# Deferring the norm's factor: branch projections of the raw x, scaled on VectorE afterwards

## The chip, the cores and the metric

The kernel runs as one program on one core of a Trainium2 chip. The metric is the device time of one execution in microseconds (us). Three runs of the kernel before gave 3948.61, 3948.72 and 3963.4 us, median 3948.72 us. One further execution was recorded by the profiler.

## The reference, cut to what matters

Two blocks run after each other on x (1024 tokens, width 1024). The change lies where the first hands x to the second.

```python
x = x + gate[:, None] * y                    # end of the first block, y = (...) @ w_out[1]

def rmsnorm(x, g):
    return x * lax.rsqrt(jnp.mean(x * x, axis=-1, keepdims=True) + RMS_EPS) * g

h = rmsnorm(x, g_mix)                        # start of the second block
z = h @ w_in                                 # the branch projections
q, k, v, f = split(z[..., :FOX_COLS])        # q, k: rmsnorm per head of 64; f: 8 logits
zr = z[..., FOX_COLS:FOX_COLS + RWKV_COLS]
zr = zr + mu_shift * (token_shift(zr) - zr)  # needs the token before
r, kr, vr, dw, da, dg = split(zr)
decay = exp(-exp(-softplus(-(w0 + tanh(dw) @ w_decay_up)) - 0.5))
a = sigmoid(a0 + da @ w_aaa_up)
kk = kr * k_k / max(sqrt(sum(kr * k_k squared)), 1e-12)     # per head
kr = kr * (1 + (a - 1) * k_a)
bonus = sum(r * kr * r_k) * vr
gates = sigmoid(z[..., FOX_COLS + RWKV_COLS:])              # 2048 columns
```

The norm's factor is one number per token, so it can be applied to x ahead of the product or to the product's output.

## The kernel before

All arrays lie feature-major: 128 features on the partitions, tokens along the free axis. Every float32 operand of a large product is parted into a rounded high part and a low rest, and a product is three matmuls: high by high, high weights by low x, low weights by high x. A tile of 128 output features takes 8 parts of x (k), two halves of 512 tokens (c) and three matmuls, 48 in all.

**End of the first block.** `gemm_residual` multiplies eight tiles of `w_out`. Per tile VectorE adds the result to x (L502), ScalarE stores x (L529) and squares it (L533), and VectorE adds the squares up (L494). After the last tile TensorE takes the mean of the squares per token (L471), ScalarE the root (L538), VectorE the reciprocal (L516). `end_section` (L159) then holds all engines together.

**Start of the second block.** `branches` begins in `norm`. TensorE spreads the factor over the partitions (L2588), ScalarE copies it to SBUF (L2680), VectorE makes u = x * gain * factor (L2785), ScalarE rounds u (L2683), VectorE (L2788) and GpSimd (L2568) subtract for the low part. SyncE loads the first weight tiles (L2521), then some twenty small operands (L2526), for which VectorE waits. GpSimd parts the weight tiles (L2562, L2564). TensorE fills its wait with `keep_busy` matmuls (L166).

**The 84 chunks.** 42 tiles (4 value, 4 query, 4 key, 14 "shifted" for the rwkv branch, 16 gates) make 84 chunks of 512 tokens, numbered s = 0 to 83, with 24 matmuls each. A list written out by hand, `order`, gives every engine the same sequence: `gemm` s, what is set "after" it, `keep` s, what is set "late" after it. A chunk's four psum regions are reused every fourth chunk, so `gemm` s waits for `keep` s-4. GpSimd parts tile j+2 after both chunks of tile j are multiplied.

In `keep` ScalarE empties the psum: for value, query and key by one copy; for a shifted chunk by a copy to `raw` (L2701) and a scaled copy (L2702), after which VectorE adds the shifted part (`shift`, L2816); for a gate by a sigmoid (L2708), which SyncE stores.

Eight **preparations** i = 0 to 7 of the rwkv operands begin at chunk s = 34 + 3i. TensorE: `low` after chunk s (L2642), `ksum` after s+1 (L2650), `rksum` after s+4 (L2655). ScalarE: in `rates`, late in s, a square and two sigmoids (L2740 to L2743); in `decay`, late in s+1, a root (L2746) and three exponentials (L2751 to L2753). VectorE: in `rates` a running sum and a subtraction (L2822, L2824); in `decay` a maximum, a reciprocal (L2831), kk (L2833) and four more (L2836 to L2841); in `products`, late in s+2, one product (L2847); in `bonus`, late in s+4, one product (L2851). GpSimd: in `products` four products (L2574 to L2580), the first of which waits for kk.

Of the kernel before, what the change touches and what calls it, by code (L numbers as in the profile page):

```python
# [21 lines left out]
P = 128  # L22
# [187 lines left out]
class Ahead:  # L210


    def __init__(self, pg, st, nk, tiles):
        self.pg, self.tiles = pg, tiles
        self.raw = pg.sbuf(st, "weights", [P, 2, nk, P])
        self.hi, self.lo = pg.pair(st, "weights", [P, 2, nk, P])

    def begin(self):

        self.loaded = [self.pg.sem("ahead_loaded") for _ in range(2)]  # L220
        self.rounded, self.parted = self.pg.sem("ahead_rounded"), self.pg.sem("ahead_parted")

    def fetch(self, queue):
        for b in range(2):
            queue.dma_start(self.raw[:, b], self.tiles(b)).then_inc(self.loaded[b], 16)

# [195 lines left out]
def gemm_residual(pg, cn, w_of, n, rhs, x, parts, nk, store=None, squares=None, maker_in=None, beside_in=None, x_source=None, ahead=None):  # L422
# [7 lines left out]
    with ExitStack() as st:  # L430
        w = Weights(pg, st, nk, ahead)
        maker = maker_in(st) if maker_in else None
        beside = beside_in(st) if beside_in else None
        acc_ready, acc_free, stored = pg.sem("acc_ready"), pg.sem("acc_free"), pg.sem("stored")
# [5 lines left out]
        with nc.Block() as block:  # L440
            @block.sync
            def _(sp):
# [12 lines left out]
                elif maker:  # L455
                    with sp.Fori(1, n // 2) as i:
                        for b in range(2):
                            sp.wait_ge(w.parted, 2 * i + b + 1)
                            sp.dma_start(w.raw[:, b], in_turn(w_of)(i, b)).then_inc(w.loaded[b], 16)

            @block.tensor
            def _(pe):
                multiply(pg, pe, w, rhs, pg.acc, chunks, nk, acc_ready, acc_free, n, maker=maker, beside=beside)
                if squares:
# [10 lines left out]
            def _(pool):  # L475
# [3 lines left out]
                part_weights(nc, pool, w, acc_ready, n)  # L479

            @block.vector
            def _(dve):
# [13 lines left out]
                for t in range(n):  # L496
                    dve.wait_ge(acc_ready, t + 3)
# [7 lines left out]
                    if squares and t >= 2:  # L505
# [5 lines left out]
                if squares:  # L511
# [8 lines left out]
            def _(act):  # L520
# [5 lines left out]
                for t in range(n if store is not None or squares else 0):  # L526
# [9 lines left out]
                if squares:  # L536
                    act.wait_ge(mean_ready, 1)
                    nc.scalar.activation(pg.rstd[:, 0:width // P], pg.aux[:, 0, 0:width // P], ACT.Sqrt, bias=cn["eps"][:]).then_inc(rms_ready, 1)  # L538
                if store is not None:
                    act.wait_ge(stored, 16 * n)  # L540
# [1527 lines left out]
def first_block(pg, cn, x_dram, arena):  # L2068
# [3 lines left out]
    with ExitStack() as both:  # L2072
# [23 lines left out]
        for l in range(DEPTH):  # L2096
# [10 lines left out]
            with early, ExitStack() as feats:  # L2107
                h = pg.pair(feats, "h", [P, KD, TOK])
# [3 lines left out]
                if not last:  # L2112
# [4 lines left out]
                              beside_in=None if last else next_in, ahead=ahead)  # L2117
            pg.end_section()

# [263 lines left out]
def branches(pg, cn, x, names, cols, conv, ops, tail, end_decay, minus_c, drams):  # L2383
# [63 lines left out]
    for s in range(n_first, 2 * n):  # L2447
        j, c = divmod(s, 2)
        order.append(("gemm", s))
        order += at_slot.get((s, "after"), [])  # L2450
        order.append(("keep", s))
        if kinds[j][0] == "shifted":
            order.append(("shift", s))
            if j < first_shifted + 2:
                order.append(("squash", s))
# [10 lines left out]
    with ExitStack() as st:  # L2466
        hi, lo = pg.pair(st, "h", [P, KD, SEQ])
        raw_w = pg.sbuf(st, "weights", [P, 2, KD, P])
        w_hi, w_lo = pg.pair(st, "weights", [P, 2, KD, P])
# [3 lines left out]
        sig, rate, total, cur, inv, prev, sq = (temps[:, i] for i in range(7))  # L2473
        bonus = tail[:, 0:2 * BANK].rearrange("p (r n) -> p r n", n=BANK)
# [8 lines left out]
        u, rstd_all = ops[:, 1:3], tile(3)  # L2483
# [6 lines left out]
        x_scaled, x_rounded, even_parted, odd_parted = pg.sem("x_scaled"), pg.sem("x_rounded"), pg.sem("even_parted"), pg.sem("odd_parted")  # L2490
# [3 lines left out]
        raw_ready, shifted, squashed = pg.sem("raw_ready"), pg.sem("shifted"), pg.sem("squashed")  # L2494
# [4 lines left out]
        bonus_stored = [pg.sem("bonus_stored") for _ in range(2)]  # L2499
# [1547 lines left out]
```

## Time and profile before

| | us |
|---|---|
| median of three runs | 3948.72 |
| profiled execution, its own time | 3957.22 |
| span of its trace | 3955.3 |
| TensorE busy | 3662.7 (93%) |
| VectorE busy | 2009.4 (51%) |
| GpSimd busy | 1862.1 (47%) |
| ScalarE busy | 1210.5 (31%) |

Read the busy shares as averages over stages with different limits. The stage that the change touches runs from about 1769 us (last section of the first block) to about 2382 us (end of `branches`). A row of a timeline is: start, duration, engine, line, operation, output<-inputs, count, and in brackets the idle time ahead of it with what ended it. Float32 matmuls on unparted operands appear as two records each.

### The profile page before, as it was taken

The page shows a single profiled execution, that of the slowest core. Times are in us where ns is not written, and L with a number is a line of the kernel's source. Part 1 is how long each engine was busy: PE and PEld are TensorE (multiplying, and loading weights), DVE is VectorE, ACT ScalarE, POOL GpSimd, SP SyncE. Part 2 cuts the span into 40 slices and gives each one's busy share as a digit, 9 for nine tenths or more (in the row PEclk, how much of TensorE's full clock was granted, in tenths as well). Part 3 has the DMA queues.
Part 4 walks back from the last instruction along what each step waited for, and adds up shares of the span by engine and source line. Part 5 has one row for each costly group of instructions (what it writes and reads, how often), then busy time and mean ns, then how long its engine had stood idle before and what let it go on. Part 6 is the DMA issues. An engine that isn't in the chain of part 4 may idle for free. (4 is left out here: it accounts for less than half of the span.)

```text
span 3955.3 us, 61428 instructions
## 1 busy us (share of the span) xinstructions
PE 3662.7 (93%) x26042; PEld 2780.3 (70%) x26042; DVE 2009.4 (51%) x2267; ACT 1210.5 (31%) x1720; POOL 1862.1 (47%) x1046
## 2 busy tenths in 40 slices
PE   6999899889899999889999997788989899999998
PEld 5888544678778644677777786676567788887877
DVE  4433576562543566543449403435643588884242
ACT  3123344431213344421235312223511344441020
POOL 1332266543333266443336535321543599993433
PEclk9999899999999999999999999998999999999999
DMA  4111200035111100031211220002023122225211
GB/s 184 32 39 67 66 1 1 26 118 187 59 32 70 37 1 1 26 128 60 91 64 48 88 78 14 4 15 84 1 88 136 64 80 85 87 89 173 73 48 69
DMA packets 101958, 258.55 MB, mean 65 GB/s; under 512 B 29232, under 2 KB 38576, under 8 KB 100800
## 3 DMA queue, kind: packets, MB, share of 16 engines
q1 hardware_dynamic: 82864, 215.03, 15.7%
q10 hardware_dynamic: 18832, 39.72, 3.0%
q8 instruction: 202, 3.31, 0.4%
q14 instruction: 60, 0.49, 0.0%
HBM read 200.16 MB, written 54.56 MB: 64 GB/s over the span
## 5 line engine op out<-in xcount | busy, mean ns | idle before, releaser
L1816 PE MATMUL acc<-h_hi,weights_hi 128*128 128x512 f32 (+1 forms) x928 | 364.9, 393 | 9.8 <-DVE h_lo L1977 7.4
L1063 DVE TENSOR_REDUCE part_max<-aux 128x1 f32<-128x428 f32 (+5 forms) x468 | 252.9, 581 | 179.5 <-PE aux L904 127.8
L1818 PE MATMUL acc<-h_hi,weights_lo 128*128 128x512 f32 (+1 forms) x928 | 339.8, 366 | 0.0
L1817 PE MATMUL acc<-h_lo,weights_hi 128*128 128x512 f32 (+1 forms) x928 | 339.4, 366 | 0.0
L2507 PE MATMUL acc<-h_hi,weights_hi 128*128 128x512 f32 x672 | 274.3, 408 | 12.1 <-POOL weights_lo L2564 6.7
L1855 POOL TENSOR_TENSOR weights_hi<-weights,ones 128x1024 fp32r<-128x1024 f32 x42 | 80.4, 1914 | 433.1 <-PE acc L1818 391.2
L1991 DVE RECIPROCAL arena<-arena 128x512 f32<-128x512 f32 (+1 forms) x48 | 141.7, 2953 | 262.2 <-ACT arena L1954 262.2
L2509 PE MATMUL acc<-h_hi,weights_lo 128*128 128x512 f32 x672 | 263.9, 393 | 0.0
L2508 PE MATMUL acc<-h_lo,weights_hi 128*128 128x512 f32 x672 | 263.5, 392 | 0.0
L1025 ACT ACTIVATE probs<-acc 128x1024 f32<-128x1024 f32 (+1 forms) x168 | 168.4, 1003 | 252.7 <-PE acc L939 252.1
L950 PE MATMUL acc<-probs,v_tok 128*64 128x512 f32 (+3 forms) x864 | 223.2, 597 | 2.2 <-DVE inverse L1083 2.2
L1816 PEld LDWEIGHTS acc<-h_hi,weights_hi 128*128 128x128 f32 x928 | 175.8, 189 | 52.3 <-issue 20.3
L3682 PE MATMUL acc<-operand_hi,weights_hi 128*128 128x512 f32 x504 | 197.3, 391 | 10.6 <-POOL weights_lo L3421 10.6
L1817 PEld LDWEIGHTS acc<-h_lo,weights_hi 128*128 128x128 f32 x928 | 175.9, 190 | 40.4 <-issue 13.4
L3683 PE MATMUL acc<-operand_lo,weights_hi 128*128 128x512 f32 x504 | 197.0, 391 | 0.0
L3684 PE MATMUL acc<-operand_hi,weights_lo 128*128 128x512 f32 x504 | 197.0, 391 | 0.0
L1818 PEld LDWEIGHTS acc<-h_hi,weights_lo 128*128 128x128 f32 x928 | 175.7, 189 | 28.9
L2562 POOL TENSOR_TENSOR weights_hi<-weights,ones 128x1024 fp32r<-128x1024 f32 x42 | 84.0, 2000 | 233.1 <-PE acc L2509 203.8
L938 PE MATMUL acc<-q_both_parts,k_twice 128*128 128x512 f32 (+3 forms) x432 | 188.8, 438 | 1.4 <-ACT q_and_shift L997 1.2
L1134 POOL TENSOR_TENSOR total<-total,probs 128x1024 f32<-128x1024 f32 (+1 forms) x72 | 159.1, 2210 | 35.7 <-ACT probs L1022 17.0
L939 PE MATMUL acc<-q_and_shift,k_rest_and_one 65*128 65x512 f32 (+3 forms) x432 | 166.7, 387 | 0.0
L2507 PEld LDWEIGHTS acc<-h_hi,weights_hi 128*128 128x128 f32 x672 | 127.3, 189 | 51.9 <-issue 23.3
(517 smaller groups left out, 9116.3 us busy)
## 6 DMA issues: line engine op xcount, KB each, us to landing
weights<-in_w_in SPq DMA_DIRECT2D x44, 512.0 KB, 3.5
arena<-in_w_mod SPq DMA_DIRECT2D x6, 2048.0 KB, 8.8
weights<-in_w_up SPq DMA_DIRECT2D x24, 512.0 KB, 4.4
weights<-in_w_out SPq DMA_DIRECT2D x22, 512.0 KB, 5.2
weight_sums<-feed_forward_spill SPq DMA_DIRECT2D x22, 512.0 KB, 4.4
xT<-in_w_up SPq DMA_DIRECT2D x20, 512.0 KB, 4.4
weights<-in_w_mod SPq DMA_DIRECT2D x4, 2048.0 KB, 26.5
mixer_gates<-arena SPq DMA_DIRECT2D x32, 256.0 KB, 2.0
```

Source lines behind the costliest of these rows:

```text
L938: nc.tensor.matmul(tile[:, hh], twice[:, at], qs[:, p % 2, hh, cols], start=True, stop=False)
L950: mm = nc.tensor.matmul(outs[blk % 2][halves[hh], skip:qn], pairs[p].v(t, hh), probs[:, e % ring, hh, skip:qn], start=i == 0, stop=e == bl ...
L1063: nc.vector.tensor_reduce(part_max[:, b % 2, j, hh, i:i + 1], max_tile(m)[:, hh, 0:cw], AX_X, ALU.max, negate=True).then_inc(max_done, 1)
L1816: nc.tensor.matmul(out, w_hi[:, b, k, :], hi[:, k, cols], start=(k == 0), stop=False)
L1817: nc.tensor.matmul(out, w_hi[:, b, k, :], lo[:, k, cols], start=False, stop=False)
L1818: return nc.tensor.matmul(out, w_lo[:, b, k, :], hi[:, k, cols], start=False, stop=(k == KD - 1))
L2507: nc.tensor.matmul(out, w_hi[:, b, k, :], hi[:, k, at], start=(k == 0), stop=False)
L2508: nc.tensor.matmul(out, w_hi[:, b, k, :], lo[:, k, at], start=False, stop=False)
L2509: return nc.tensor.matmul(out, w_lo[:, b, k, :], hi[:, k, at], start=False, stop=(k == KD - 1))
L3682: nc.tensor.matmul(out, w.hi[:, o, j, :], operands[0][:, o, j, :], start=start, stop=False)
L3683: nc.tensor.matmul(out, w.hi[:, o, j, :], operands[1][:, o, j, :], start=False, stop=False)
L3684: return nc.tensor.matmul(out, w.lo[:, o, j, :], operands[0][:, o, j, :], start=False, stop=stop)
```

## The change

1. `h` = x * gain only. ScalarE rounds it (hi, with the gain as scale), VectorE makes lo from x, gain and hi. The factor is applied when a chunk leaves the psum: `keep` moves from ScalarE to VectorE, one multiplication by the factor `rstd_of[c]` for each of the 84 chunks. A shifted chunk goes to `raw` that way, and ScalarE makes the scaled copy from `raw`; `shift` and `squash` of chunk s now stand in `order` ahead of `keep` s+1. A gate goes to `raw` and ScalarE applies the sigmoid there. The forget logits get their factor on VectorE too.
2. The last `gemm_residual` of the first block (`late`) leaves out the store, the square and the sum of tile 7, and mean, root and reciprocal. They are done inside `branches`: TensorE takes the mean after three of the eight parts of x, and spreads the factor after chunk 2.
3. The first two weight tiles are loaded and parted during that `gemm_residual` (`following`), with the gain column.
4. `norm` multiplies tile 0 part by part, then tile 1 whole; ahead of it `keep_busy` is 20 instead of 44, and `keep_busy` of 8 ahead of chunk 4 is gone. GpSimd no longer takes part in `norm`.
5. `bonus` has one buffer instead of two, and `prev` shares `sig`: `decay` i waits for the store of bonus i-1, `rates` i for the product i-1.

```diff
-    order = [("split", 0), ("split", 1), ("load", 2), ("load", 3), ("norm", 0)]
-    order += [("keep", s) for s in range(n_first)]
-    order += [("split", 2), ("load", 4), ("split", 3), ("load", 5)]
+    order = [("load", 2), ("load", 3), ("norm", 0), ("keep", 0), ("keep", 1), ("split", 2), ("load", 4)]
+    order += [("keep", 2), ("keep", 3), ("split", 3), ("load", 5)]
...
         order += at_slot.get((s, "after"), [])
+        if kinds[(s - 1) // 2][0] == "shifted":
+            order.append(("shift", s - 1))
+            if (s - 1) // 2 < first_shifted + 2:
+                order.append(("squash", s - 1))
         order.append(("keep", s))
-        if kinds[j][0] == "shifted":
-            order.append(("shift", s))
...
# TensorE, norm
-                    keep_busy(pg, pg.acc[:, 0], 44)
+                    keep_busy(pg, pg.acc[:, 1], 20)
+                    for k in range(KD):
+                        pe.wait_ge(x_parted, k + 1)
+                        for c in range(2):
+                            mm = product(pg.acc[:, 0, c * BANK:(c + 1) * BANK], 0, k, c)
...
+                        if k == 2:
+                            pe.wait_ge(squared, 1)
+                            for t in range(SEQ // P):
...
# ScalarE, norm and keep
+                    for k in range(KD):
+                        nc.scalar.activation(hi[:, k], x[:, k], ACT.Copy, scale=cols["g_mix_2"][:, k:k + 1]).then_inc(x_rounded, 1)
...
-                            nc.scalar.copy(raw[:, 1 + c * BANK:1 + (c + 1) * BANK], acc).then_inc(raw_ready, 1)
-                            nc.scalar.activation(part(region, c), acc, ACT.Copy, scale=keep_mu[:, region:region + 1]).then_inc(kept, 1)
+                            act.wait_ge(kept, i + 1)
+                            nc.scalar.activation(part(region, c), raw[:, 1 + c * BANK:1 + (c + 1) * BANK], ACT.Copy,
+                                                 scale=keep_mu[:, region:region + 1]).then_inc(level_ready, 1)
...
-                            nc.scalar.activation(stage[:, c], acc, ACT.Sigmoid).then_inc(kept, 1)
+                            act.wait_ge(kept, i + 1)
+                            nc.scalar.activation(stage[:, c], stage[:, c], ACT.Sigmoid).then_inc(gate_made, 1)
...
# VectorE, keep and norm
+                    dve.wait_ge(acc_ready, i + 1)
+                    tt(dst, pg.acc[:, j % 2, c * BANK:(c + 1) * BANK], rstd_of[c], ALU.mult).then_inc(kept, 1)
...
+                    for k in range(KD):
+                        dve.wait_ge(x_rounded, k + 1)
+                        stt(lo[:, k], x[:, k], cols["g_mix_2"][:, k:k + 1], full(hi[:, k]), ALU.mult, ALU.subtract).then_inc(x_parted, 1)
...
-                        stt(u[:, k % 2], x[:, k], cols["g_mix_2"][:, k:k + 1], rstd_all, ALU.mult, ALU.mult).then_inc(x_scaled, 1)
```

**What moves in the preparations.** VectorE, kernel before, from kk of preparation 0 (chunk 35) to the maximum of preparation 1 (chunk 38); L2816 is `shift`:

```order
L2833 SCALAR_TENSOR_TENSOR arena<-arena,k_k_16,temps 128x512
L2836 TENSOR_SCALAR temps<-temps,k_a_17 128x512
L2837 SCALAR_TENSOR_TENSOR arena<-temps,arena 128x512
L2840 SCALAR_TENSOR_TENSOR arena<-arena,r_k_18 128x512
L2841 COPY end_decay<-temps 128x8
L2816 SCALAR_TENSOR_TENSOR arena<-raw,mu_shift_21,arena 128x512
L2847 SCALAR_TENSOR_TENSOR arena<-arena,temps 128x512
L2816 SCALAR_TENSOR_TENSOR arena<-raw,mu_shift_21,arena 128x512
L2822 SCALAR_TENSOR_TENSOR temps<-arena,temps 128x512
L2824 TENSOR_TENSOR temps<-temps 128x512
L2816 SCALAR_TENSOR_TENSOR arena<-raw,mu_shift_21,arena 128x512
L2851 SCALAR_TENSOR_TENSOR arena<-aux,arena 128x512
```

The same place of the changed kernel, from the copy that ends `decay` 0 on; L2857 is `shift`, L2820 the new `keep`, L2863 the running sum of preparation 1, L2871 its maximum:

```order
L2882 COPY end_decay<-temps 128x8
L2857 SCALAR_TENSOR_TENSOR arena<-raw,mu_shift_21,arena 128x512
L2820 TENSOR_TENSOR raw<-acc,arena 128x512
L2888 SCALAR_TENSOR_TENSOR arena<-arena,temps 128x512
L2857 SCALAR_TENSOR_TENSOR arena<-raw,mu_shift_21,arena 128x512
L2820 TENSOR_TENSOR raw<-acc,temps 128x512
L2863 SCALAR_TENSOR_TENSOR temps<-arena,temps 128x512
L2865 TENSOR_TENSOR temps<-temps 128x512
L2857 SCALAR_TENSOR_TENSOR arena<-raw,mu_shift_21,arena 128x512
L2820 TENSOR_TENSOR raw<-acc,arena 128x512
L2892 SCALAR_TENSOR_TENSOR arena<-aux,arena 128x512
L2871 TENSOR_SCALAR temps<-temps 128x512
```

A `keep` stands directly ahead of the running sum and directly ahead of `bonus` and the maximum; `shift` is that of the chunk before.

ScalarE, kernel before, from chunk 37 (`rates` 1) to the root of `decay` 1:

```order
L2701 COPY raw<-acc 128x512
L2702 ACTIVATE arena<-acc,one_minus_mu 128x512
L2740 ACTIVATE temps<-arena,k_k_16 128x512
L2742 ACT_TABLE_LOAD
L2742 ACTIVATE temps<-acc,w_2_14 128x512
L2743 ACTIVATE temps<-acc,a_2_15 128x512
L2701 COPY raw<-acc 128x512
L2702 ACTIVATE arena<-acc,one_minus_mu 128x512
L2746 ACT_TABLE_LOAD
L2746 ACTIVATE temps<-aux 128x512
```

The same place of the changed kernel; L2732 is the scaled copy of chunks 36 and 37, then of 38:

```order
L2732 ACTIVATE arena<-raw,one_minus_mu 128x512 x2
L2767 ACTIVATE temps<-arena,k_k_16 128x512
L2769 ACT_TABLE_LOAD
L2769 ACTIVATE temps<-acc,w_2_14 128x512
L2770 ACTIVATE temps<-acc,a_2_15 128x512
L2732 ACTIVATE arena<-raw,one_minus_mu 128x512
L2773 ACT_TABLE_LOAD
L2773 ACTIVATE temps<-aux 128x512
```

The psum copy of each chunk is gone from ScalarE; what is left at its head, L2732, reads `raw`, which VectorE writes in `keep`.

## Rows read from the trace of the kernel before

**Rows 1.** The page: span, then busy time, share and instructions of each engine.

```profile
span 3955.3 us, 61428 instructions
PE 3662.7 (93%) x26042; PEld 2780.3 (70%) x26042; DVE 2009.4 (51%) x2267; ACT 1210.5 (31%) x1720; POOL 1862.1 (47%) x1046
```

**Rows 2.** Busy time by stretch: length, PE, PEld, DVE, ACT, POOL, PEclk, DMA, GB/s.

```profile
1824.80:1880.40 55.60, 45.41 (x253) 40.25 (x251) 27.53 (x21) 14.53 (x17) 22.21 (x11) 0.88 0.20 60
1880.40:2067.60 187.20, 187.13 (x810) 148.82 (x810) 82.78 (x50) 50.44 (x80) 69.98 (x33) 1.00 0.24 79
2067.60:2235.70 168.10, 162.78 (x666) 121.55 (x666) 146.04 (x105) 89.72 (x124) 113.58 (x57) 0.99 0.18 58
```

**Rows 3.** Timeline of TensorE between the two blocks.

```profile
1823.41 0.39 PE L319 MATMUL acc<-h_hi,weights_hi 128*128 128x512 f32 x1
...
1824.77 2.39 PE L166 MATMUL aux<-dense 128*128 128x128 f32 x20
1829.03 1.95 PE L471 MATMUL aux<-mean,arena 128*128 128x1 f32 x16 [1.87 <-DVE arena L494]
1832.59 3.75 PE L2588 MATMUL aux<-ident,rstd_by_token 128*128 128x128 f32 x16 [1.61 <-PEq L159]
...
1852.42 0.77 PE L2507 MATMUL acc<-h_hi,weights_hi 128*128 128x512 f32 x1 [5.41 <-DVE h_lo L2788]
...
1880.47 0.50 PE L2507 MATMUL acc<-h_hi,weights_hi 128*128 128x512 f32 x1 [1.38 <-POOL weights_lo L2564]
```

**Rows 4.** Timeline of VectorE between the two blocks.

```profile
1824.97 1.28 DVE L502 SCALAR_TENSOR_TENSOR arena<-acc,mod,arena 128x1024 f32<-128x1024 f32 x1 [8.46 <-PE acc L321]
...
1831.31 0.20 DVE L516 RECIPROCAL rstd_by_token<-rstd_by_token 128x8 f32<-128x8 f32 x1 [2.34 <-ACT rstd_by_token L538]
1848.66 2.48 DVE L2785 SCALAR_TENSOR_TENSOR arena<-arena,g_mix 128x1024 f32<-128x1024 f32 x2 [17.14 <-DMA b_f<-in_b_f]
```

**Rows 5.** Groups by line: busy us, mean ns of one, idle before.

```profile
L2683 ACT CAST h_hi<-arena 128x1024 fp32r<-128x1024 f32 x8 | 8.4, 1051 | 24.3 <-DVE arena L2785 23.9
...
L2851 DVE SCALAR_TENSOR_TENSOR arena<-aux,arena 128x512 f32<-128x512 f32 x8 | 5.5, 682 | 9.4 <-PE aux L2655 9.4
```

**Rows 6.** Busy time by stretch, four us after a stall of TensorE.

```profile
2158.00:2162.00 4.00, 4.00 (x12) 3.07 (x11) 4.00 (x4) 1.67 (x3) 3.92 (x2) 0.61 0.47 146
```

**Rows 7.** Timeline of VectorE, from kk of preparation 0 to kk of 2.

```profile
2082.96 0.75 DVE L2833 SCALAR_TENSOR_TENSOR arena<-arena,k_k,temps 128x512 f32<-128x512 f32 x1
...
2087.49 0.74 DVE L2816 SCALAR_TENSOR_TENSOR arena<-raw,mu_shift,arena 128x512 f32<-128x512 f32 x1
...
2089.85 1.78 DVE L2816 SCALAR_TENSOR_TENSOR arena<-raw,mu_shift,arena 128x512 f32<-128x512 f32 x1
2091.55 2.91 DVE L2822 TENSOR_TENSOR_SCAN temps<-arena,temps 128x512 f32<-128x512 f32 x1
...
2097.14 0.74 DVE L2816 SCALAR_TENSOR_TENSOR arena<-raw,mu_shift,arena 128x512 f32<-128x512 f32 x1
...
2102.23 0.75 DVE L2833 SCALAR_TENSOR_TENSOR arena<-arena,k_k,temps 128x512 f32<-128x512 f32 x1
...
2124.69 0.75 DVE L2833 SCALAR_TENSOR_TENSOR arena<-arena,k_k,temps 128x512 f32<-128x512 f32 x1
```

**Rows 8.** Timeline of ScalarE in preparations 1 and 2.

```profile
2094.17 1.28 ACT L2746 ACT_TABLE_LOAD   x1
2095.46 0.60 ACT L2746 ACTIVATE temps<-aux 128x512 f32<-128x512 f32 x1
...
2108.67 0.73 ACT L2740 ACTIVATE temps<-arena,k_k 128x512 f32<-128x512 f32 x1
```

**Rows 9.** Timeline of TensorE: the longest stall, and the last `rksum`.

```profile
2157.73 0.47 PE L2507 MATMUL acc<-h_hi,weights_hi 128*128 128x512 f32 x1 [2.69 <-POOL weights_lo L2564]
...
2234.82 1.02 PE L2655 MATMUL aux<-arena,head_mean 128*128 128x512 f32 x2
```

**Rows 10.** Timeline of GpSimd: the parting that begins where that of tile 30 ends.

```profile
2235.21 1.89 POOL L2562 TENSOR_TENSOR weights_hi<-weights,ones 128x1024 fp32r<-128x1024 f32 x1
```

More of the change, by code:

```diff
@@ L210, with __init__ @@
 class Ahead:
[L213 to L216, printed above, removed]
+    def __init__(self, pg, st, nk, tiles, raw=None, side="left", extra=()):
+        self.pg, self.tiles, self.extra = pg, tiles, extra
+        self.raw = pg.sbuf(st, "weights", [P, 2, nk, P]) if raw is None else raw
+        self.hi, self.lo = pg.pair(st, "weights", [P, 2, nk, P], side)
     def begin(self):
@@ L433, in gemm_residual @@
         beside = beside_in(st) if beside_in else None
+        if following:
+            following.begin()
+        n_here = n - 1 if late else n
         acc_ready, acc_free, stored = pg.sem("acc_ready"), pg.sem("acc_free"), pg.sem("stored")
@@ L463, in _ @@
                 multiply(pg, pe, w, rhs, pg.acc, chunks, nk, acc_ready, acc_free, n, maker=maker, beside=beside)
-                if squares:
+                if squares and not late:
                     if not beside:
@@ L479, in _ @@
                 part_weights(nc, pool, w, acc_ready, n)
+                if following:
+                    for b in range(2):
+                        following.low(pool, b)
+                    pool.wait_ge(following.parted, 2)
             @block.vector
@@ L496, in _ @@
                 for t in range(n):
+                    if late and t >= 2:
+                        add_squares(t - 1)
                     dve.wait_ge(acc_ready, t + 3)
@@ L504, in _ @@
                     up.then_inc(acc_free, 1)
-                    if squares and t >= 2:
+                    if squares and t >= 2 and not late:
                         add_squares(t - 1)
@@ L525, in _ @@
                     maker.scalar(act)
-                for t in range(n if store is not None or squares else 0):
+                for t in range(n_here if store is not None or squares else 0):
                     act.wait_ge(acc_free, t + 3)
@@ L535, in _ @@
                         beside.keep(act, t - 2)
-                if squares:
+                    if following and t in (4, 5):
+                        following.high(act, t - 4)
+                if squares and not late:
                     act.wait_ge(mean_ready, 1)
@@ L2472, in branches @@
         sq_ring, rstd_ring = temps[:, 0:2], temps[:, 2:4]
-        sig, rate, total, cur, inv, prev, sq = (temps[:, i] for i in range(7))
-        bonus = tail[:, 0:2 * BANK].rearrange("p (r n) -> p r n", n=BANK)
+        sig, rate, total, cur, inv, sq = (temps[:, i] for i in range(6))
+        bonus, rstd_of = tail[:, 0:BANK], [tail[:, BANK:2 * BANK], temps[:, 6]]
         raw = pg.sbuf(st, "raw", [P, 1 + SEQ])
```

200 lines of the change are left out of this document (110 added, 90 removed).

## The prediction

> **What bounds the kernel now.** I read the page first: TensorE is busy for 93% of the span [rows 1], so time is to be had only where it waits. Then the stretches of the stage that changes [rows 2]: from 1880.4 to 2067.6 TensorE is busy for 187.13 of 187.20 us and nothing else can matter there. Two other stretches lose time. Between the blocks, 55.6 us, it is busy for 45.4, and most of that is filler, mean and spreading; the timeline shows it [rows 3]. In the preparations, 2067.6 to 2235.7, it is busy for 162.8 of 168.1 us, and VectorE for 146.0: there VectorE is nearly full, and where TensorE stops it waits for GpSimd's weight tiles (three stalls of 1.98, 2.69 and 0.66 us; the longest in [rows 9]), which GpSimd parts after its products, which wait for kk of VectorE. So in the preparations the chain is VectorE, GpSimd, TensorE. The change takes work out of the first stretch and puts work and waits on VectorE in the second.
>
> **Part 1, between the blocks: what goes.** Measure from filler's start at 1824.77, where the products of w_out end, to chunk 4 at 1880.47: 55.7 us [rows 3]. In it today: filler, mean, root, reciprocal, barrier, spreading, and a wait of VectorE of 17.14 us for the small operands [rows 4].
>
> After: the last update of x ends at 1824.97 + 1.28 = 1826.25 [rows 4]. From the end of the reciprocal (1831.51) to TensorE's first work behind the barrier (1832.59) are 1.1 us [rows 3, 4], so the new block begins at 1827.3. Filler 20 is twice the ten that took 2.39 us: 4.8 us, until 1832.1. The first part of x is ready before that: 1.05 us of rounding on ScalarE [rows 5] and 1.24 us for the low part (two took 2.48 without GpSimd beside them [rows 4]) give 1829.6. After that VectorE delivers a part each 1.24 us, while TensorE takes 6 matmuls each. Six matmuls take 1.36 us (1823.41 to 1824.77 [rows 3]), so x keeps ahead. Chunks 0 to 3 are 96 matmuls of 0.227 us: 21.8 us. In between, the mean now has 16 products, of which 8 took 1.95 us: 3.9 us; and the spreading, 3.75 us at half clock, 1.9 us at full clock. Chunk 4 begins at 1832.1 + 21.8 + 3.9 + 1.9 = 1859.7. Its weights: the parting of tile 2 starts after chunk 1 at about 1847 and takes some 4.3 us; the small operands (14 us of issuing from 1827.3) have landed by 1845. Both are covered. Gain 1880.47 - 1859.7 = 20.8 us.
>
> The clock can take some back. TensorE idles 2.5 us ahead of the filler. [...] A half-rate stretch as in rows 6 costs 1.6 us, one of 6 us costs 3. I take 1.3: **-19.5 us**, bounds -20.8 and -17.5.
>
> Preparing the first weight tiles a stage ahead (two roundings on ScalarE, two low parts on GpSimd, two loads) I cost at nothing: TensorE is alone bound there, and the two engines have gaps of over 5 us in each 10.9 us tile. Without that cover each would cost its 2 us once.
>
> **Part 2, the 84 `keep`s on VectorE.** The nearest row is L2851, also one psum and one SBUF input of 128x512: 0.68 us [rows 5], 0.60 to the next start. Outside the preparations VectorE waits for chunks, so 60 of them are hidden; with the 24 of the preparations it is otherwise. Follow one preparation from the end of kk, t = 0 (2083.6 [rows 7]).
>
> Before: four operations until 3.9 (2087.49), `shift`, product and `shift` until 7.9 (2091.55), sum and subtraction until 13.5 (2097.14), `shift`, `bonus`, maximum, reciprocal, kk until 19.3. ScalarE is never late there: it emptied each chunk by itself and ran ahead.
>
> After: 3.9 as before; then `shift`, `keep`, product, `shift`, `keep`: 4.06 as in the rows and two `keep`s, 1.2: 9.1. Now comes what the diff hides. ScalarE's sigmoid for the running sum stands behind its scaled copy of the same chunk, which waits for this last `keep`. So after 9.2 come 0.6 copy, 0.74 square, 1.28 table load, 0.69 sigmoid (load and square in [rows 8]): VectorE starts the sum at 12.5, not 9.1. The same happens at chunk s+1: the root for the maximum stands behind the copy that waits for `keep`. That `keep` and its latency 0.74, copy 0.7, table load 1.29, root 0.6 make 3.3 us from `keep` to maximum [rows 8], where `bonus` fills 0.6.
>
> Some comes back. After even preparations GpSimd is done at about t = 12.2, and sum and subtraction, 5.6 us beside it [rows 7], take 1.9 us alone. So: 12.5 + 1.9 + `shift` 0.7 = 15.1, + 3.3 = 18.4, + maximum, reciprocal and kk 4.5 = 22.8, against 19.3 (2102.23 minus 2082.96). After odd ones GpSimd parts two tiles, until 17.4, and sum and subtraction stay slow (4.9): 12.5 + 4.9 + 0.7 + 3.3 + 4.5 = 25.9, against 22.5 (2124.69 minus 2102.23). **Each preparation is 3.5 us longer.** kk of preparation 0 does not move, since VectorE was idle ahead of it; kk of 7 comes 7 x 3.5 = 24.5 us later. The two preparations beside gate chunks have no `shift` but a sigmoid in the copy's place, and I leave them at the same price.
>
> Is TensorE hit in full? Before, `rksum` 7 starts at 2234.82 and takes 0.86, so chunk 60 could begin at 2235.7, and its weights came at 2235.2 [rows 9, 10]: slack 0.5. So 24.0. The stalls grow to some 5 us each, and the clock drop behind the last one is new: +1.7 as in rows 6. Together **+25.7 us**. Bounds: below 0, if the longer gaps of VectorE and GpSimd give back as much contention as they cost; above 38, by the price of contended `keep`s below. I take the walk, since all its terms but the copy from SBUF are durations of rows.
>
> [...] L2851 keeps its 0.68 us also where GpSimd runs beside it, while the SBUF-only `shift` goes from 0.74 to 1.78 [rows 5, 7]. [...]
>
> [...] Rows 8 show 1.29 us from load to root. [...]
>
> **Part 3, the small ones.** The waits for the store of `bonus` and for the product i-1 are covered: some 7 us lie between `bonus` and the next write to its buffer, and the product is done before `keep` allows the sigmoid. If the store took longer than 7 us it would add what is over. The forget logits block VectorE's `keep`s for 25 us after chunk 64; `gemm` 69, the first that needs one of them, comes 7 us later. The last chunk leaves by `keep` and sigmoid instead of a sigmoid: **+0.7 us**.
>
> **Sum.** -19.5 + 25.7 + 0.7 = +6.9 us. The profiled execution took 3957.22 us, 1.9 more than its span and 8.5 more than the median, so it would take 3964; a median near 3948.7 + 6.9 = 3955.6, say 3956 us.
>
> **Rivals.**
> (a) *VectorE absorbs it.* If ScalarE's copy costs no wait, a preparation grows only by three `keep`s, 1.8 us, and the relief (3.7 us in even steps) outweighs that; TensorE would lose 0 to 5 us more. Time: 3948.7 - 19.5 + 3 = 3932. For it: 22 us of VectorE are idle in 168 [rows 2]. Against it: nearly all of that lies before kk of 0 and after the last `shift`, and the order rows put the copy ahead of the sigmoid.
> (b) *Slower: `keep` contends with GpSimd.* If it takes 1.78 us as `shift` does, 1.1 more, with two of three beside GpSimd's work: 2.2 us per preparation, 15 in seven, +22 in all: 3971. It decides if `keep` exceeds about 1.5 us. Against it: L2851.
> (c) *The gap does not close as it should.* If the clock is at half through the whole filler, that takes 9.6 us instead of 4.8, and with some first matmuls at half rate the gain is 14 instead of 19.5: 3961. For it: the spreading of rows 3 ran at half rate (3.75 us) after a short idle. Against it: the last products before the gap are dense.
> (d) *The table load is dearer behind a wait*, by one more load of 1.28 us: two in each of seven steps, +18: 3974. [...] Against it: both loads of rows 8 and the root right behind.
>
> **How the numbers follow.** A difference below 0.5%, 19.7 us, this kernel's runs cannot tell from none; so the bounds are 3929.0 and 3968.5. The walk, 0.58 (own range 3944 to 3968); (a) 0.18; (b) 0.11; (c) 0.10; (d) 0.03. Faster than 3929 needs (a) with its cost at or below zero: 0.09. Slower than 3968.5 is (b), (d) and a tail of the walk: 0.15. Within: 0.76. The range 3932 to 3971 takes in (a) and (b).
>
> **What would show it.** Right: chunk 4 begins some 34 to 37 us after the last product of w_out; VectorE idles about 3 us ahead of each running sum and 2 us ahead of each maximum, released by ScalarE; its kk's lie 23 and 26 us apart; TensorE stalls of 4 to 6 us on GpSimd's low weights. (a) would show kk's 19 to 22 us apart. (b) would show L2820 near 1.8 us. (c) would show a granted clock of 0.5 in the first chunks. I am wrong at the root if ScalarE's copies run ahead of VectorE, or if chunks outside the preparations wait for `keep`.

## The result, and the profile after

*Before* and *after* name the two kernels from here on; a_... are variants of after, b_... variants of before.

The kernel after takes 3981.26 us (median of 6 runs, 3972.52 to 3987.85), the kernel before in the same comparison 3958.86 us (3948.61 to 3963.68). The ratio is 1.0053, with a 95% interval of 1.0036 to 1.0071: 21 us slower, where 7 were forecast. The profiled execution has 3980.65 us, 23.4 more than that of before (3957.22).

The page, as [rows 1]: span, then busy time, share and instructions.

```profile
span 3978.8 us, 61312 instructions
PE 3681.7 (93%) x25974; PEld 2786.4 (70%) x25974; DVE 2041.6 (51%) x2348; ACT 1184.4 (30%) x1668; POOL 1846.4 (46%) x1040
```

The three stretches of [rows 2], cut at the same events: end of the last product of `w_out`, chunk 4, first `low`, chunk 60.

```profile
1821.00:1860.50 39.50, 37.08 (x186) 31.84 (x185) 13.69 (x18) 12.10 (x13) 4.30 (x2) 0.87 0.26 71
1860.50:2051.50 191.00, 191.00 (x809) 148.86 (x808) 100.48 (x81) 31.66 (x48) 70.54 (x32) 1.00 0.22 75
2051.50:2243.00 191.50, 169.12 (x665) 121.50 (x665) 143.78 (x132) 81.76 (x106) 108.62 (x57) 0.97 0.15 51
```

The first is 16 us shorter (55.6), the third 23 longer (168.1), both near the forecast. But the middle one, in which TensorE does the same work without a pause, takes 191.0 us instead of 187.2. That is the first surprise: of this stretch the prediction said that TensorE is busy throughout and nothing else can matter.

TensorE between the blocks, as [rows 3]:

```profile
1820.84 0.39 PE L326 MATMUL acc<-h_hi,weights_lo 128*128 128x512 f32 x1
1823.65 6.19 PE L166 MATMUL acc<-dense 128*128 128x128 f32 x40 [2.42 <-PEq L159]
1829.59 0.48 PE L2535 MATMUL acc<-h_hi,weights_hi 128*128 128x512 f32 x1
...
1837.71 0.77 PE L2535 MATMUL acc<-h_hi,weights_hi 128*128 128x512 f32 x1
1838.28 0.63 PE L2536 MATMUL acc<-h_lo,weights_hi 128*128 128x512 f32 x1
...
1853.15 1.95 PE L2634 MATMUL aux<-ident,rstd_by_token 128*128 128x128 f32 x16
```

The filler takes 6.19 us, not 4.8, and the 15 products behind the mean start 0.43 us apart: the granted clock is down, 0.80 of full speed from 1821.0 to 1829.6 us and 0.58 from 1837.7 to 1845.0.

VectorE, and below it ScalarE, from the running sum to kk of preparation 1, as [rows 7, 8]:

```profile
2075.28 0.68 DVE L2820 TENSOR_TENSOR raw<-acc,temps 128x512 f32<-128x512 f32 x1
2079.42 1.22 DVE L2863 TENSOR_TENSOR_SCAN temps<-arena,temps 128x512 f32<-128x512 f32 x1 [3.46 <-ACT temps L2769]
...
2085.53 0.43 DVE L2871 TENSOR_SCALAR temps<-temps 128x512 f32<-128x512 f32 x1 [2.17 <-ACT temps L2773]
...
2089.38 0.75 DVE L2874 SCALAR_TENSOR_TENSOR arena<-arena,k_k,temps 128x512 f32<-128x512 f32 x1
```

```profile
2076.05 0.72 ACT L2732 ACTIVATE arena<-raw,one_minus_mu 128x512 f32<-128x512 f32 x1 [2.55 <-DVE raw L2820]
...
2077.40 1.28 ACT L2769 ACT_TABLE_LOAD   x1
2078.70 0.69 ACT L2769 ACTIVATE temps<-acc,w 128x512 f32<-128x512 f32 x1
```

One sees the walk of the prediction: `keep` ends at 2075.96, ScalarE's copy (L2732) follows, square, table load, sigmoid, and only then starts the sum, after 3.46 us of idling. In all preparations (columns: us in total, times, longest):

```profile
DVE temps L2863 <- ACT temps L2769: 23.1, 8, 3.5
DVE temps L2871 <- ACT temps L2773: 17.6, 8, 2.8
```

The same two waits of VectorE, for the sigmoid and for the root, in before:

```profile
DVE temps L2822 <- ACT temps L2742: 4.9, 5, 1.9
DVE temps L2830 <- ACT temps L2746: 1.6, 2, 1.0
```

The kk's of preparations 0 to 7 lie 22.7, 26.4, 22.6, 26.4, 22.6, 23.2 and 20.3 us apart. `keep` keeps its price:

```profile
L2820 DVE TENSOR_TENSOR raw<-acc,arena x30: 671/692/694, 1994.8 to 2385.6; 128x512 f32<-128x512 f32 x30
```

(ns least, median, most; first and last start.) TensorE has three stalls of about 5 us. The last, of chunk 60, is on GpSimd's low weights, and the clock granted behind it is low, 0.57 of full speed from 2243.0 to 2247.0 us, as the 0.61 in [rows 6]:

```profile
2243.03 0.63 PE L2535 MATMUL acc<-h_hi,weights_hi 128*128 128x512 f32 x1 [4.93 <-POOL weights_lo L2592]
2243.45 0.63 PE L2536 MATMUL acc<-h_lo,weights_hi 128*128 128x512 f32 x1
```

The other two are not what the prediction named: there `ksum` (L2682) waits for ScalarE's square (L2767), which also stands behind the scaled copy. One of them, and the totals of both waits from the first `low` up to chunk 60:

```profile
2126.45 2.07 PE L2682 MATMUL aux<-temps,head_mean 128*128 128x512 f32 x2 [4.96 <-ACT temps L2767]
```

```profile
PE aux L2682 <- ACT temps L2767: 14.4, 5, 5.0
PE acc L2535 <- POOL weights_lo L2592: 3.1, 3, 1.1
```

Laid end to end, the two profiled executions differ so: up to the last product of `w_out` -3.7 us; from there to the last product of `branches` +16.4 (553.8 to 570.2); TensorE's pause behind it +0.7 (4.42 to 5.09); the scan (`rwkv_scan`, not touched by the change), first to last product, +12.2 (281.4 to 293.7); the rest -2.1. The head, up to chunk 4, is 16.2 us shorter in it (39.7 us for 55.9). Of the eleven variants of after, whose code there does the same work, nine take 38.2 or 38.3 us for it and two 36.7, so the size of this gain holds within 3 us only. Two things had to be explained beyond the forecast: products of this stage that start every 233 ns instead of 227, and a scan that is longer though its code is the same.

### The profile page after: what moved, and what is told of

It is laid out like the page before. It is cut to its first block and busy times, and to the rows that moved or that the text cites. A ratio compares the mean times of both kernels' runs of the same rounds, so it can differ in the third digit from the quotient of the medians.

```text
span 3978.8 us, 61312 instructions
## 1 busy us (share of the span) xinstructions
PE 3681.7 (93%) x25974; PEld 2786.4 (70%) x25974; DVE 2041.6 (51%) x2348; ACT 1184.4 (30%) x1668; POOL 1846.4 (46%) x1040
## 5 line engine op out<-in xcount | busy, mean ns | idle before, releaser
L1050 ACT ACTIVATE probs<-acc 128x1024 f32<-128x1024 f32 (+1 forms) x168 | 168.6, 1004 | 254.3 <-PE acc L964 252.6
## 6 DMA issues: line engine op xcount, KB each, us to landing
weights<-in_w_mod SPq DMA_DIRECT2D x4, 2048.0 KB, 26.4
```

## The experiments

Stage is below the time from the last product of `w_out` to the last of `branches`: 553.8 us before, 570.2 after. Scan is the time from its first to its last product. Ratios are to the kernel before, with 95% intervals.

### 1. Why 233 ns: where the weight tiles lie

**b_right**, the kernel before with the pair at the other end of SBUF:

```
-        w_hi, w_lo = pg.pair(st, "weights", [P, 2, KD, P])
+        w_hi, w_lo = pg.pair(st, "weights", [P, 2, KD, P], "right")
```

> The kernel before, with only the weight pair of branches allocated on the right side (weights_hi at byte 221152 of a partition, weights_lo at 212960, as in the kernel after; before: 192928 and 201120; temps and raw move down). Theory P (the products' spacing of 233.3 ns in the kernel after comes from where the weight tiles lie in SBUF): products of branches start every 233 ns, 84 chunks of 24 take 0.15 us longer each, +12 to +13 us, ratio to before 1.0032. Theory V (the spacing comes from VectorE reading psum in keep beside the products): spacing stays 227 ns, ratio 1.000.

Products of TensorE in before, and below them in b_right; the first column is the start:

```profile
2351.64 0.39 PE L2507 MATMUL acc<-h_hi,weights_hi 128*128 128x512 f32 x1
2351.87 0.39 PE L2508 MATMUL acc<-h_lo,weights_hi 128*128 128x512 f32 x1
2352.09 0.39 PE L2509 MATMUL acc<-h_hi,weights_lo 128*128 128x512 f32 x1
```

```profile
2352.05 0.39 PE L2507 MATMUL acc<-h_hi,weights_hi 128*128 128x512 f32 x1
2352.28 0.40 PE L2508 MATMUL acc<-h_lo,weights_hi 128*128 128x512 f32 x1
2352.51 0.39 PE L2509 MATMUL acc<-h_hi,weights_lo 128*128 128x512 f32 x1
```

The mean over the stage is 233.3 ns, as in after. Stage 562.9 us, +9.1, not 12 to 13: in the preparations TensorE waits anyway, and the slower products mostly fill its waits (first `low` to chunk 60: 168.6 us, 167.8 in before). Ratio 1.0014 (0.9995 to 1.0032).

**a_low**, the kernel after with the tiles from 2 on where before has them. Tiles 0 and 1 stay, `temps` and `raw` take their place later:

```
-        w_hi, w_lo = ahead.hi, ahead.lo
+        w_hi, w_lo = pg.pair(st, "weights", [P, 2, KD, P])
...
+            of_hi, of_lo = (ahead.hi, ahead.lo) if j < 2 else (w_hi, w_lo)
```

> The kernel after, with the weight tiles from tile 2 on at 192928 and 201120, where the kernel before has them; tiles 0 and 1 stay where they were parted ahead. Theory P: products of tiles 2 and up start every 227 ns, those of chunks 0 to 3 every 233; the kernel gets 12 to 13 us faster than after, ratio to before 1.002 to 1.003. Theory V: 233 ns everywhere, ratio as after, 1.0053.

Chunks 0 to 3 have 233 ns, all others 227. Stage 560.7 us, 9.5 less than after; 1.4 of this lies in the head, where both have 233 ns, so some 8 are the spacing. Ratio 1.0045 (1.0026 to 1.0065). The ratios alone would not tell b_right from before nor a_low from after: it is the traces that show the effect. The spacing theory holds from both sides; `keep` on VectorE has no part in it.

**b_swap**, **b_high**, **b_mid** and **b_shift** ask what it is about the place. All are the kernel before with its allocations in another order (`w_lo, w_hi = ...`; the pair behind `raw`; `raw` ahead of the pair; `temps` and `raw` ahead of `h`).

> The kernel before, the low weight tiles at 192928 and the high ones at 201120 (exchanged). If the order of the two decides, the products of branches start every 233 ns; if where the pair lies in SBUF decides, every 227 ns.

> The kernel before, the weight pair allocated behind temps and raw: high tiles at 211392, low ones at 219584, their order as in before. If the place decides (high addresses, or the distance to h at 119200 and 151968), 233 ns; if the order decides, 227 ns.

> The kernel before, raw allocated ahead of the weight pair: high tiles at 197056, low at 205248, 4128 bytes higher, so that their distance to h (119200, 151968) is no longer a multiple of 8192. If the distance to h decides the spacing, products start every 233 ns; if an absolute place above about 211000 does, every 227 ns.

> The kernel before, temps and raw allocated ahead of h: everything from h on lies 18464 bytes higher (h at 137664 and 170432, weights at 211392 and 219584), the distances between h and weights as in before. If the distance decides, 227 ns; if the absolute place of the weights does, 233 ns as in b_high.

| kernel | h_hi, h_lo at byte | weights_hi, _lo at | step of products |
|---|---|---|---|
| before | 119200, 151968 | 192928, 201120 | 227 ns |
| b_swap | same | 201120, 192928 | 227 |
| b_mid | same | 197056, 205248 | 233 |
| b_high | same | 211392, 219584 | 233 |
| after, b_right | same | 221152, 212960 | 233 |
| b_shift | 137664, 170432 | 211392, 219584 | 227 |

One trace of each was taken; the step is the mean over the products at full clock. b_high, then b_shift:

```profile
2351.71 0.40 PE L2508 MATMUL acc<-h_lo,weights_hi 128*128 128x512 f32 x1
2352.41 0.40 PE L2508 MATMUL acc<-h_lo,weights_hi 128*128 128x512 f32 x1
```

```profile
2351.92 0.39 PE L2508 MATMUL acc<-h_lo,weights_hi 128*128 128x512 f32 x1
2352.60 0.39 PE L2508 MATMUL acc<-h_lo,weights_hi 128*128 128x512 f32 x1
```

(Three products lie between the starts of two such rows: 0.70 and 0.68 us.) b_high and b_shift have the weights at the same bytes; of the operands of a product only `h` lies elsewhere. So not the address of the weights but their distance to the other operand decides. In the fast ones each distance is a multiple of 8192 bytes (73728, 81920, 40960, 49152); in the slow ones 4128, 2080 or 3648 bytes are over. The 3648 of b_right are a multiple of 64, so that is not enough; between that and 8192 the step that matters is open, and so is the reason. What the place is worth in these traces is 6 ns a product.

### 2. The hand-over in the preparations

**a_copylate** and **a_copylate2**: the kernel after, with ScalarE's scaled copy behind the stage's late items in its own order:

```
+    act_order = list(order)
+    for q in range(len(order) - 1):
+        if act_order[q][0] == "keep" and act_order[q + 1][0] in ("rates", "decay", "bonus"):
+            act_order[q], act_order[q + 1] = act_order[q + 1], act_order[q]
```

a_copylate lacks `"bonus"`, an item without work for ScalarE that stands between `keep` and all `decay`s but the first.

> The kernel after, with ScalarE's scaled copy of a shifted chunk behind the rates or decay items of the same slot in ScalarE's order. Theory H (the hand-over keep, copy, then sigmoid and root is what lengthens the preparations): kk's spacing falls from 23 and 26 to 20 and 23 us, the first low product to chunk 60 takes about 170 us instead of 191.5, the kernel is 20 us faster than after, ratio to before 1.000. Rival B (VectorE has no room for keep, 3 x 0.6 us per preparation, whatever ScalarE's order): the stretch gets at most 5 us shorter, ratio 1.004 to 1.005.

It came halfway: kk's 22.2 and 23.7 us apart, first to last `low` 154.8 us (160.8 in after, 143.0 before), stage 557.0, ratio 1.0029 (1.0016 to 1.0042). Its waits show what was left:

```profile
DVE temps L2875 <- ACT temps L2777: 15.7, 8, 2.2
DVE temps L2867 <- ACT temps L2773: 5.8, 8, 1.2
```

The sum (L2867) waits 17 us less, the maximum (L2875) nearly as long as in after (17.6 us). TensorE's wait for the square has fallen from 14.4 us to 1.2, and its wait for GpSimd's low weights, the one that the prediction named, has grown from 3.1:

```profile
PE acc L2539 <- POOL weights_lo L2596: 10.7, 3, 4.7
```

> As a_copylate, but the scaled copy also moves behind decay where a bonus item stands between them: in a_copylate only the first decay was freed, and VectorE still waited 2.0 us for the root in each of the other seven preparations. Theory H (hand-over): these 2.0 us go too, 12 to 14 us; kk's lie 18 to 21 us apart, first low product to last low product 142 to 146 us (154 in a_copylate, 160 in after, 142.5 before), the kernel 10 us faster than a_copylate. Rival B (VectorE and GpSimd are full): it stays within 3 us of 154.

```profile
DVE temps L2867 <- ACT temps L2773: 5.6, 8, 1.0
DVE temps L2875 <- ACT temps L2777: 1.6, 2, 0.8
```

kk's 20.0 and 22.5 us apart, `low`s 144.8 us, stage 546.0: 24.2 us less than after. Ratio 1.0002 (0.9981 to 1.0022). From the first `low` to chunk 60 it takes 170.0 us (191.5 in after, 167.8 before): of the 23.7 us by which the preparations had grown, ScalarE's order made 21.5. With it mended the 24 `keep`s on VectorE cost 0.7 us in each of the early even steps and nothing in the odd ones (19.3 and 22.5 before).

**a_both** (a_low and a_copylate) and **a_all** (a_low and a_copylate2):

> Both edits. By P and H together 32 us faster than after, ratio to before 0.997; TensorE then reaches chunk 60 about 167 us after the first low product, and the 16 us won between the blocks stay won.

> Low weight tiles and the scaled copies behind rates and decay: first to last low product 142 us or less, branches from its first product to its last 528 us (545.5 before, 540 in a_both), ratio to before 0.997 to 0.998 if the scan after it keeps its 10 us loss.

Stage 549.1 and 534.2 us; ratios 1.0008 (0.9992 to 1.0024) and 0.9970 (0.9953 to 0.9988). a_all is faster than both kernels. Its stage is 19.6 us shorter than that of before: what the new head is worth when nothing is paid for it.

### 3. The scan behind the stage

By the stage alone after would be 16 us slower, and a_all 20 faster. By the ratios they are 21 slower and 12 faster: in after and the five variants of it above, 5 to 11 us are lost elsewhere (8 in the mean). The profiled executions put it in the scan, where work is equal and the granted clock is not. Before and after:

```profile
2382.70:2664.20 281.50, 222.14 (x8604) 196.98 (x8604) 112.64 (x176) 70.37 (x135) 111.90 (x88) 0.97 0.02 6
```

```profile
2396.10:2689.80 293.70, 234.57 (x8604) 207.66 (x8604) 115.25 (x175) 70.66 (x135) 112.03 (x88) 0.92 0.02 6
```

First theory, C: the longer pause ahead of the scan. **a_all_fill** fills it, **b_gap** makes it in the kernel before:

```
+                pe.wait_ge(minus_kept, 1)
+                keep_busy(pg, pg.aux[:, 0], 14)
```

```
+                                nc.scalar.copy(stage[:, c], acc).then_inc(last_copied, 1)
+                                act.wait_ge(last_copied, 1)
+                                acc = stage[:, c]
```

> a_all with 14 filler products of TensorE behind the last chunk of branches. Theory C (the longer pause of 5.1 us before the scan leaves TensorE at half clock for 10.5 to 11.7 us and brings on the 20 us at half clock near the scan's end, which every variant of after shows and before does not): with a pause of about 2 us the scan takes 278 to 283 us instead of 290 to 295; ratio to before 0.994 to 0.995. Rival D (the clock near the scan's end has nothing to do with the pause): the scan's first 10 us get faster by at most 4 us, its end stays at half clock, ratio 0.997.

> The kernel before, whose last gate chunk is first copied and then put through the sigmoid in place, so that the end of branches is 0.7 us later, as in the kernel after; nothing else is changed. Theory C: the pause of TensorE grows from 4.4 to 5.1 us, the scan takes 290 us or more instead of 281, ratio 1.002 to 1.003. Rival D: 0.7 us, ratio 1.000, scan 280 to 283 us.

C fell. b_gap has the pause of 5.09 us and a scan of 280.4; a_all_fill has no gain (0.9973, 0.9956 to 0.9991) and a scan of 296.8. b_gap's ratio is 1.0011 (0.9994 to 1.0027).

Second theory, E: every 126 products or so TensorE pauses in the middle of a run of products. The profile names "issue" there, that is, nothing that it waited for. The changed program has 34 TensorE instructions fewer ahead of the scan, so that these pauses fall elsewhere. Before, then after; the count at the end of a row says how much of its run of 64 was left:

```profile
2396.12 1.03 PE L2965 MATMUL acc<-arena 64*64 64x64 f32 x53 [0.40 <-issue]
2400.04 1.04 PE L2983 MATMUL acc<-inverse_t,level 64*64 64x64 f32 x55 [0.78 <-issue]
```

```profile
2416.49 1.03 PE L3010 MATMUL acc<-arena 64*64 64x64 f32 x51 [0.84 <-issue]
2420.41 1.03 PE L3019 MATMUL acc<-p,inverse 64*64 64x64 f32 x53 [0.63 <-issue]
```

Counted from the scan's first product, the marked pauses stand at 339, 465, 592 before and at 533, 659, 912 after. **b_10** takes 34 fillers out of the kernel before (44 to 10 ahead of chunk 0), **a_all_34** adds 34 short products behind the last chunk of a_all:

> The kernel before with a filler of 10 instead of 44 products ahead of the first chunks of branches: TensorE has 34 instructions fewer ahead of the scan, as in the kernel after. Theory E: the scan's issue gaps move to where after has them, and it takes 288 us or more, +8; ratio 1.002 or more. Rival F: scan 279 to 284 us; whatever else changes lies at the head of branches, where the clock may stay at half for the first chunks.

> a_all with 34 short TensorE products (16 columns each) behind the last chunk of branches, in its pause before the scan. The kernel after has 34 TensorE instructions fewer ahead of the scan than the kernel before (9849 against 9883); TensorE's gaps of about 1 us without a releaser (issue) then fall on other instructions of the scan. Theory E (where these gaps fall decides whether the clock drops to half near the scan's end): with the count as before, the scan takes 279 to 284 us (281.4, 279.4 and 280.4 in before, b_right, b_gap) instead of 288 in a_all, and its issue gaps stand at the instructions of before; ratio to before 0.994 to 0.996. Rival F (something else in the changed kernel lowers the clock): scan 285 us or more.

b_10's pauses stand at 533, 912, 1038, as in after, its scan takes 292.6 us at a clock of 0.92, and while its stage is 1.8 us shorter than that of before, its ratio is 1.0020 (1.0003 to 1.0037), 8 us slower. That speaks for E. a_all_34 was a poor test: its pauses are at 339 and 465, but the 34 products took 11.4 us, put the scan off by 7.5, and its end ran at half clock (0.50 granted) for 44 us (scan 299.6; ratio 0.9983, 0.9967 to 0.9999).

**a_w34** and **a_all_w34** add waits that are long over instead, twice 34 calls, which make 34 instructions:

> The kernel after, with waits on a semaphore that is already reached behind the last chunk of branches, so many that TensorE's program has 34 instructions more ahead of the scan, 9883 as in the kernel before; no work is added, and they run in TensorE's pause of 5.1 us. Theory E (the position of TensorE's instructions, and with it of its issue gaps and of the delayed masks, costs the scan some 8 to 12 us): issue gaps of the scan stand where before has them (products 339, 465, 592, ...), the masks land in about 3.5 us instead of 4.6, the scan takes 279 to 286 us; 8 us faster than after, ratio to before 1.003. Rival F (the scan's loss is chance or has another cause): ratio as after, 1.005, scan 290 us or more.

> The same waits in a_all. Theory E: ratio to before 0.995 (a_all 0.997), scan 279 to 286 us instead of 288. Rival F: 0.997, as a_all.

Ratios 1.0059 (1.0035 to 1.0083) and 0.9978 (0.9962 to 0.9994): no gain. But the pauses had moved to 515 and 642 only, 17 or 18 products: a filler product counts for four such waits. The pages count them so too: 61292 instructions in b_10 against 61428 in before, 136 fewer for 34 products; 61347 in a_w34 against 61312 in after, 35 more for 34 waits. **a_pos** and **a_all_pos** add 132 of them, in TensorE's waits, so that the stage is as long as without (569.7 and 534.2 us):

```
+                        if i in (3, 5):
+                            for _ in range(96):
+                                pe.wait_ge(x_rstd, 2)
                         pe.wait_ge(kk_sq_ready, i + 1)
```

> The kernel after with 132 wait instructions of TensorE on a semaphore long reached: 96 in its two pauses of 4.96 us in the preparations, 36 behind the last chunk. a_w34 moved the scan's issue gaps by only 17 to 18 products (a 128x128 f32 product is four instructions on the engine, a wait is one); 132 should bring them to within two products of those of before (339, 465, 592, ...). Theory E: start of the scan as before (masks 3.5 us, first two groups of products 4.3 us apart), scan 279 to 292 us, and over all runs 7 us faster than after, ratio 1.0035 to 1.004. Rival F: same ratio as after and a_w34, 1.0053 to 1.0059.

> The same 132 in a_all, 60 and 30 in its two longest pauses (3.46 and 1.86 us ahead of products that wait for weights) and 42 behind the last chunk. Theory E: ratio 0.995 to 0.9955; rival F: 0.997 to 0.998.

The pauses are within two products of those of before (594, 1098, 1224; 592, 1097, 1223 there). Ratios 1.0032 (1.0019 to 1.0044) against 1.0053 and 1.0059, and 0.9960 (0.9944 to 0.9975) against 0.9970 and 0.9978: 8 and 4 us less with instructions that do nothing. The intervals overlap, so neither pair shows the effect by itself.

Taken over all kernels with several runs it is clearer. From the time that a kernel's ratio gives, take what its stage and its pause ahead of the scan have changed, both by its trace. In the ten kernels whose pauses stand elsewhere (after, b_10, a_low, a_both, a_all, a_all_fill, both copylates, both w34) 4 to 10 us are left, 7.4 in the mean. In the five where they stand as in before (b_right, b_gap, a_all_34, a_pos, a_all_pos) it is -4 to 4, 0.6 in the mean. Kernels of both families are in both groups. One such value is good to 5 to 10 us either way, by the ratios' intervals, so only the groups tell.

The window of a_pos's scan:

```profile
2400.85:2679.32 278.47, 219.98 (x8604) 194.72 (x8604) 113.51 (x175) 70.53 (x135) 111.87 (x88) 0.99 0.02 6
```

One part of the mechanism shows at the scan's start, where VectorE waits for the masks, a transfer. After and a_pos:

```profile
2401.49 1.29 DVE L3165 TENSOR_TENSOR ab_t<-acc,arena 128x512 f32<-128x512 f32 x2 [4.73 <-DMA arena<-in_c_scan]
```

```profile
2404.27 1.29 DVE L3170 TENSOR_TENSOR ab_t<-acc,arena 128x512 f32<-128x512 f32 x2 [2.80 <-DMA arena<-in_c_scan]
```

It is 3.96 in b_10, 2.85 in before and b_gap. This is 1 to 2 us; the rest goes with the granted clock over the scan, 0.97 in before, 0.92 in after and b_10, 0.99 in a_pos. Over all profiles the scan takes 278.5 to 291.7 us (mean 283.5 of 9) where the pauses are as in before, 284.5 to 296.8 (290.8 of 10) where they are not; a_all_34, whose own products put the scan off, is left out (with it 285.1 of 10). So the mean moves by 7 us, as the ratios do, but single executions overlap: near its end the scan runs at half clock (0.50 granted) for anything from 0 to 44 us, 7 in before, 20 in after, 0 in a_pos, but 31 in b_high and b_mid, whose scan and pauses are those of before. Of the 12 us between the two profiled executions about 5 would be such chance. How a pause's place could bring the clock down near the end was not found; that the pauses' place is the cause rests on b_10, a_pos and a_all_pos and on the two groups, not on a mechanism.

## Why the prediction was wrong

The sum gave 3956 us with a range up to 3971, and after came at 3981. Of these 25 us, 10 are the base: the sum was put on three runs of before with a median of 3948.7, and six have 3958.9. On that base the same sum gives 3966 and the range ends at 3981. The change itself was forecast at 7 us and cost 21 by the ratio. By the terms:

**Part 1, -19.5: right in mechanism, taken back in part.** The new block began 2.4 us behind `w_out`, the mean took 3.8 us, the spreading 1.95, and the small operands were in time. Chunk 4 began 39.5 us after the products of `w_out`. The sum had 34.9 and 1.3 for the clock; the clock cost some 4 (1.1 in the filler, 2.9 in 15 products), and the spacing 0.6. Net -16.2, less than the bounds of -20.8 and -17.5 allowed; nine of the variants of after had 1.4 us more. Rival (c) had this direction and in part this size. Up to the first `low` the gain is 17.7 us in a_low, 19.3 in a_all.

**Part 2, +25.7: right on VectorE and in size, wrong on where TensorE waits.** kk's 22.7 and 26.4 us apart (22.8 and 25.9 forecast); the stretch from the first `low` to chunk 60 grew by 23.7, where the sum had 24.0; taking the hand-over away gave 24.2 us in after and 26.5 in a_low. Both waits of the walk are there, at the sum and at the maximum: a_copylate took away the first with 13 us, a_copylate2 the second with 11. The two together, 40.7 us, are more than the growth: before, VectorE already waited 6.5 us there, and the sum and the subtraction, beside GpSimd less often, fell from 37.7 us to 28.1, the relief that the walk had (the sum of preparation 1 took 2.91 us beside GpSimd in [rows 7], 1.22 in after, where GpSimd's parting ends 0.13 us into it). What it had wrong is the last link. It took every stall of TensorE to be on GpSimd's low weights; two of the three long ones were `ksum` waiting for the square. The sum did not need it, as it was put on the spacing of the kk's, and that spacing and the growth of the stretch agree (23.7 us each). That TensorE follows VectorE by either wait is argued from this, not tested. Chunk 60 began at 2235.40 in before, so the slack taken as 0.5 us was 0.2. Rival (a) fell with that, and (b) by `keep`'s 0.69 us beside GpSimd. (d) fell too: 1.30 us from the table load's start to the sigmoid's (2077.40 to 2078.70), not one load more. The walk, with 1.28 us a load, met the spacing of the kk's.

**Part 3, +0.7: right.** The pause grew from 4.42 to 5.09 us.

**The failing step is the price of a product.** "Chunks 0 to 3 are 96 matmuls of 0.227 us", and no term for the others: the sum took the rate of [rows 3] over to a kernel whose weight tiles lie elsewhere. The text on the change does not say it, but one word of the new kernel does, where the first weight tiles are allocated ahead:

```
+        after = lambda raw: Ahead(pg, begun, KD, weight_tiles(ins["w_fox"], 2 * FOX_TILES * P), raw, "right", [(cols["g_mix_2"][:], ins["g_mix_2"])])
```

It cost 8 to 9 us in the stage (9.1 in b_right), more than the whole net forecast of 6.9. The prediction had looked for waits alone: where TensorE is busy for 187.13 of 187.20 us "nothing else can matter there", and there it lost 3.9 us. None of the rivals held it. By stretch, from start to start of the products named: head -16.2, chunk 4 to the first `low` +3.9 (191.0 for 187.1), preparations +23.7 (191.5 for 167.8), chunk 60 to the end +5.1 (148.0 for 142.9, with some 1.6 for the clock behind the last stall). Together these are the 16.4 measured.

**The other missing term lies outside the stage.** The sum assumed that unchanged code keeps its time. With 34 TensorE instructions fewer ahead of it the scan took some 7 us more, in the mean of its executions. The forecast's 7, with 9 and 7 more, is 23, against 21 (14 to 28) measured; the terms themselves are known to 3 us at best, so part of this agreement is luck. The net forecast was the small difference of two terms of about twenty, and either omission is as large as it.

## What to carry to other kernels

When a change moves an allocation, compare the start-to-start step of a long run of products before and after, and try streamed operand and weights a multiple of 8192 bytes apart: that gave the shorter step in every kernel here, though a smaller multiple may do. When work leaves one engine for another, walk the order of the engine that it leaves: an item that now waits holds up what stands behind it, and putting it behind the urgent items gave 24 us here. When the net of a forecast is smaller than the scatter of the runs, take more runs for its base: three were 10 us off. And when unchanged code gets slower, look at where the pauses marked "issue" fall and at the granted clock, over several executions, before looking for a cause in the change.

## What was not expected of the hardware

The step of a 128x512 product in f32 was 227 or 233 ns by the distance between its operands in SBUF alone. With instructions that do nothing, in places where TensorE waits anyway, the kernel after came out 8 us faster, by intervals that overlap. And the scan, with the same code in every kernel, ran in 278.5 to 299.6 us, most of it by the clock that it was granted: 0.99 of full speed in the shortest (a_pos), 0.90 in the longest (a_all_34).
